# A streaming encoder step on one core: the order of the query tiles in the prompt's attention

## The chip, the cores and the metric

The kernel runs on one core of one Trainium2 chip. The core's engines work at the same time, each through its own list of instructions: TensorE (PE in the profile; its weight loads are PEld) multiplies matrices into PSUM, VectorE (DVE) and ScalarE (ACT) work elementwise and read PSUM, GpSimd (POOL) works elementwise in SBUF, and SyncE (SP) starts transfers. They meet by semaphores. The metric is the device time of the launch in microseconds (us), lower being better.

## The reference

One inference step of a two-layer encoder for a prompt of 1024 frames and eight running streams with 16 frames each. Layer 0 mixes by a gated linear recurrence, layer 1 by sparse attention, and each layer has a convolutional feed-forward part. Only the sparse attention on the prompt matters here:

```python
admissible = key_chunk[None, :] <= (pb // CHUNK)[:, None]        # chunks of 64 keys
score = jnp.where(admissible[None], score, -jnp.inf)             # from the indexer
sel_val, sel_idx = lax.top_k(score, n_sel)                       # n_sel = 256 for the prompt
logits = jnp.einsum('btkgd,btskd->btkgs', qg, kg) * scale        # 16 query heads, 4 key heads
p = jax.nn.softmax(logits, axis=-1)
o = jnp.einsum('btkgs,btskd->btkgd', p, vg)
```

A query sees its own chunk and the ones before, so a later query has more keys.

## The kernel before

The kernel is ten phases, one after the other. The phase that the diff touches, `attend_prompt_phase`, computes the prompt's attention with dense scores and a mask: `mask_p` holds 0 for the selected keys and -1e30 for the others.

The 1024 queries are eight tiles of 128 (`PT` = 8). Tile t sees (t+1) x 128 keys. The 16 heads are taken in pairs, one head in each half of the partitions, so a tile has `QB` = 8 blocks. Four blocks (`GROUP` = 4) are a group; a tile has two groups. The list `blocks` sets the order of the 64 blocks on every engine, and `groups` that of the 16 groups. Scores are written to PSUM in pieces of at most 512 keys: tiles 0 to 3 have one piece, tiles 4 to 7 have two.

A block passes the engines in this way (lines of the kernel before):

- GpSimd and ScalarE split the queries into a high and a low part (`split_q`, L2174, and L2097), six blocks ahead.
- TensorE makes the scores of both heads (`scores`, L2111 to L2115): three products a piece and head, high by high, low by high, high by low.
- VectorE adds the mask and takes the row maximum on the way out of PSUM (`maxima`, L2254), then the negative of it (`ap_neg_max`, L2263). Two pieces need one more instruction to join their maxima (L2260).
- ScalarE takes the exponentials and their sum (L2206).
- TensorE transposes the probabilities, 128 keys at a time (`turn`, L2124), and ScalarE copies them out of PSUM (L2195), two blocks (`LAG`) after the scores.
- After a whole group TensorE multiplies by the values (`values`, L2141) in parts, spread over the four blocks that follow. The sums are inverted, spread and multiplied in (L2267, L2131, L2271, L2150, L2179, L2278).

Between blocks, two searches for the top 256 are still going on, and their steps stand at fixed block numbers. Those on VectorE: twelve parts that settle the masks of tiles 6 and 7 (`finish_prompt`, in blocks 0 to 11); ten steps of the samples' search (`decide_samples`, in blocks 1 to 14, each after a pass of ScalarE over 2064 scores, `sign_samples`, L1779); and seven parts that settle the samples' mask (`finish_samples`, in blocks 28 to 34). The masks of tiles 0 to 5 are ready when the phase begins (`SEARCHED[-1]` is the pair of tiles 6 and 7).

The queries of a tile are loaded from device memory by SyncE into one of two buffers, when the tile two places before has been split.

Of the kernel before, what the change touches and what calls it, by code (L numbers as in the profile page):

```python
# [19 lines left out]
ALU = mybir.AluOpType  # L20
ACT = mybir.ActivationFunctionType
AX = mybir.AxisListType
F32 = mybir.dt.float32
# [4 lines left out]
P = 128  # L28
# [9 lines left out]
PT = NT - 1  # L38
# [29 lines left out]
class Space:  # L68
# [5 lines left out]
    def take(self, name, shape, dtype=F32, at=None):  # L74
        size = int(np.prod(shape[1:])) * (2 if dtype == BF16 else 4)
        size = (size + 31) // 32 * 32
        if at is None:
            at = self.at
            self.at += size
            assert self.at <= self.end, (name, self.at - self.end)  # L80
        t = self.nc.alloc_sbuf_tensor_at(name, list(shape), dtype, offset=at)
        t_at[name] = at
        return t
# [1064 lines left out]
GROUP = N_HEADS // N_KV  # L1148
QB = N_HEADS // 2
# [517 lines left out]
SEARCHED = (tuple(range(FIRST_TOP, FIRST_TOP + 2)), tuple(range(FIRST_TOP + 2, FIRST_TOP + 4)), tuple(range(FIRST_TOP + 4, PT)))  # L1667
# [349 lines left out]
def attend_prompt_phase(nc, env, x):  # L2017


    io, const, sem, tick = env["io"], env["const"], env["sem"], env["tick"]  # L2020
# [12 lines left out]
    q, q_hi, q_lo = take("ap_q", [P, 2, QB, P]), take("ap_q_hi", [P, QB, P], F32R), take("ap_q_lo", [P, QB, P], F32R)  # L2033
    k_hi = take("ap_k_hi", [P, 2, T_PROMPT], F32R)
    k_lo = take("ap_k_lo", [P, 2, T], F32R, at=t_at["at_k"])
# [4 lines left out]
    inv_rows, inv_of = idle("ap_inv_rows", [2 * GROUP, GROUP, P]), idle("ap_inv_of", [P, GROUP, P])  # L2040
    sel_half = idle("ap_sel_half", [2 * GROUP, P])
    own_head = take("ap_own_head", [2 * GROUP, GROUP])
    blocks = [(t, j) for t in range(PT) for j in range(QB)]
    groups = [(t, p) for t in range(PT) for p in range(2)]


    LAG, TAIL, AHEAD = 2, GROUP, QB - 2
# [8 lines left out]
    def scores_up_to(n):  # L2056
        return score_pieces[n][-1][0] + 1
# [10 lines left out]
    with ExitStack() as ctx:  # L2068
# [3 lines left out]
        q_in = [sem(f"ap_q_in{n}") for n in range(2)]  # L2072
        consts_in = sem("ap_consts_in")
        k_hi_set, q_hi_set, q_lo_set = sem("ap_k_hi_set"), sem("ap_q_hi_set"), sem("ap_q_lo_set")
# [7 lines left out]
        @block.sync  # L2082
        def _(sp):
            sp.dma_start(sel_half[:, :], io["sel_half"]).then_inc(consts_in, 16)
            sp.dma_start(own_head[:, :], io["own_head"]).then_inc(consts_in, 16)
            for t in range(PT):
                if t >= 2:
                    sp.wait_ge(q_lo_set, QB * (t - 1))
                sp.dma_start(q[:, t % 2], io["q_t"][:, :, t * P:(t + 1) * P].rearrange("j p t -> p j t")).then_inc(q_in[t % 2], 16)

        @block.gpsimd
        def _(pool):
            pool.wait_ge(k_hi_set, 1)
            pool.tensor_tensor(k_lo[:, :, 0:T_PROMPT], k_sb[:, :, 0:T_PROMPT], k_hi[:, :, :].bitcast(F32), ALU.subtract)
            for n, (t, j) in enumerate(blocks):
                pool.wait_ge(q_hi_set, n + 1)
                pool.tensor_tensor(q_lo[:, j], q[:, t % 2, j], q_hi[:, j].bitcast(F32), ALU.subtract).then_inc(q_lo_set, 1)  # L2097

        @block.tensor
        def _(pe):  # L2100
            def scores(n, c):
                t, j = blocks[n]
                k, a, e = score_pieces[n][c]
                pe.wait_ge(q_lo_set, n + 1)
                if k >= 2:
                    pe.wait_ge(qk_read, 2 * (k - 1))
                outs = [qk[half][k % 2][:, 0:e - a] for half in range(2)]
                rows = [slice(half * HEAD_D, (half + 1) * HEAD_D) for half in range(2)]
                keys = (j // GROUP, slice(a, e))
                for half in range(2):  # L2110
                    pe.matmul(outs[half], q_hi[rows[half], j, :], k_hi[(rows[half], *keys)], start=True, stop=False)  # L2111
                for half in range(2):
                    pe.matmul(outs[half], q_lo[rows[half], j, :], k_hi[(rows[half], *keys)], start=False, stop=False)
                for half in range(2):
                    i = pe.matmul(outs[half], q_hi[rows[half], j, :], k_lo[(rows[half], *keys)], start=False, stop=True)  # L2115
                i.then_inc(qk_done, 1)

            def turn(n, half):
# [49 lines left out]
        def _(act):  # L2168
            def split_q(n):
                t, j = blocks[n]  # L2170
                act.wait_ge(q_in[t % 2], 16 * (t // 2 + 1))
                if t:
                    act.wait_ge(qk_done, scores_up_to(n - QB))
                act.activation(q_hi[:, j], q[:, t % 2, j], ACT.Copy).then_inc(q_hi_set, 1)  # L2174

            def copy_inv(u):
                act.wait_ge(inv_done, u + 1)
# [4 lines left out]
            for n in range(QB):  # L2182
                split_q(n)
            for n in range(len(blocks) + LAG + TAIL):
                m, e = n - LAG, n - 1
                for half in range(2):
                    if 0 <= m < len(blocks):
                        t, j = blocks[m]
# [10 lines left out]
                    if 0 <= e < len(blocks):  # L2199
                        t, j = blocks[e]  # L2200
                        keys, u = (t + 1) * P, e // GROUP
# [604 lines left out]
```

## Time and profile before

| | us |
|---|---|
| median of three runs | 3840.33 (3840.1 to 3844.03) |
| the profiled execution | 3843.01 |
| its span | 3841.5 |
| TensorE busy in the span | 3543.3 (92%) |
| VectorE busy | 2126.6 (55%) |
| ScalarE busy | 1170.3 (30%) |
| the phase, first scores to last outputs | 2304.8 to 2607.5 |

The span is what the profiler saw between the first and the last instruction; the profiled execution's own time has some 1.5 us around it. Busy times are sums of the instructions' durations on an engine, with overlap counted once. A stretch of the span can be asked for by itself: that gives each engine's busy time in it, the number of instructions, and the clock that was granted to TensorE (1.00 is 2.4 GHz, 0.50 is 1.2 GHz). The timeline lists instructions by their start, and what an engine waited for stands in brackets.

### The profile page before, as it was taken

The page shows a single profiled execution, that of the slowest core. Times are in us where ns is not written, and L with a number is a line of the kernel's source. Part 1 is how long each engine was busy: PE and PEld are TensorE (multiplying, and loading weights), DVE is VectorE, ACT ScalarE, POOL GpSimd, SP SyncE. Part 2 cuts the span into 40 slices and gives each one's busy share as a digit, 9 for nine tenths or more (in the row PEclk, how much of TensorE's full clock was granted, in tenths as well). Part 3 has the DMA queues.
Part 4 walks back from the last instruction along what each step waited for, and adds up shares of the span by engine and source line. Part 5 has one row for each costly group of instructions (what it writes and reads, how often), then busy time and mean ns, then how long its engine had stood idle before and what let it go on. Part 6 is the DMA issues. An engine that isn't in the chain of part 4 may idle for free. (4 is left out here: it accounts for less than half of the span.)

```text
span 3841.5 us, 55603 instructions
## 1 busy us (share of the span) xinstructions
PE 3543.3 (92%) x19764; PEld 3152.8 (82%) x19780; DVE 2126.6 (55%) x3935; ACT 1170.3 (30%) x1961; POOL 224.4 (6%) x349
## 2 busy tenths in 40 slices
PE   5999999998999999999888977897889999999997
PEld 4988888986899999999853873453459999999996
DVE  5465555564555455545688666762232554555456
ACT  4222333322311111113236857673333111111112
POOL 3000000001000000002000001100002000000001
PEclk8888888887999999999958987999999999999998
DMA  2110011110111111111102220003431111111111
GB/s 89 34 40 29 30 39 40 34 40 12 41 45 44 40 45 45 39 40 55 68 12 88 70 71 23 12 1 151 160 124 41 40 43 39 45 45 40 40 45 63
DMA packets 57407, 192.23 MB, mean 50 GB/s; under 512 B 7016, under 2 KB 23408, under 8 KB 52528
## 3 DMA queue, kind: packets, MB, share of 16 engines
q1 hardware_dynamic: 52992, 167.89, 12.9%
q0 software_dynamic: 4144, 20.71, 1.5%
q8 instruction: 173, 2.83, 0.3%
q14 instruction: 98, 0.80, 0.1%
HBM read 166.64 MB, written 21.93 MB: 49 GB/s over the span
## 5 line engine op out<-in xcount | busy, mean ns | idle before, releaser
L292 PE MATMUL ff1lin<-ff1h_hi,ff1w_hi 128*128 128x384 f32 x1056 | 354.7, 336 | 9.9 <-DVE ff1w_lo L286 5.7
L292 PE MATMUL ff0lin<-ff0h_hi,ff0w_hi 128*128 128x384 f32 x1056 | 354.1, 335 | 7.2 <-DVE ff0w_lo L286 4.4
L293 PE MATMUL ff1lin<-ff1h_lo,ff1w_hi 128*128 128x384 f32 x1056 | 353.7, 335 | 0.0
L294 PE MATMUL ff1lin<-ff1h_hi,ff1w_lo 128*128 128x384 f32 x1056 | 353.6, 335 | 0.0
L293 PE MATMUL ff0lin<-ff0h_lo,ff0w_hi 128*128 128x384 f32 x1056 | 353.3, 335 | 0.0
L294 PE MATMUL ff0lin<-ff0h_hi,ff0w_lo 128*128 128x384 f32 x1056 | 353.3, 335 | 0.0
L292 PE MATMUL hg_lin<-hg_h_hi,hg_w_hi 128*128 128x384 f32 x768 | 269.6, 351 | 17.4 <-POOL hg_h_lo L165 15.4
L293 PE MATMUL hg_lin<-hg_h_lo,hg_w_hi 128*128 128x384 f32 x768 | 264.3, 344 | 0.0
L294 PE MATMUL hg_lin<-hg_h_hi,hg_w_lo 128*128 128x384 f32 x768 | 263.4, 343 | 0.0
L292 PEld LDWEIGHTS ff1lin<-ff1h_hi,ff1w_hi 128*128 128x128 f32 x1056 | 199.0, 188 | 12.7 <-DVE ff1w_lo L286 6.3
L292 PEld LDWEIGHTS ff0lin<-ff0h_hi,ff0w_hi 128*128 128x128 f32 x1056 | 198.8, 188 | 8.5 <-DVE ff0w_lo L286 4.7
L293 PEld LDWEIGHTS ff1lin<-ff1h_lo,ff1w_hi 128*128 128x128 f32 x1056 | 199.0, 188 | 0.1
L294 PEld LDWEIGHTS ff1lin<-ff1h_hi,ff1w_lo 128*128 128x128 f32 x1056 | 198.9, 188 | 0.0
L293 PEld LDWEIGHTS ff0lin<-ff0h_lo,ff0w_hi 128*128 128x128 f32 x1056 | 198.8, 188 | 0.1
L294 PEld LDWEIGHTS ff0lin<-ff0h_hi,ff0w_lo 128*128 128x128 f32 x1056 | 198.7, 188 | 0.0
L1099 DVE TENSOR_TENSOR x<-x,ff1lin 128x384 f32<-128x384 f32 x264 | 141.1, 553 | 102.3 <-PE ff1lin L294 99.9
L1099 DVE TENSOR_TENSOR x<-x,ff0lin 128x384 f32<-128x384 f32 x264 | 141.1, 553 | 101.6 <-PE ff0lin L294 99.2
L292 PE MATMUL ff1lin<-ff1y_hi,ff1w_hi 128*128 128x384 f32 x528 | 180.0, 341 | 2.5 <-DVE ff1w_lo L286 2.5
L292 PE MATMUL ff0lin<-ff0y_hi,ff0w_hi 128*128 128x384 f32 x528 | 179.9, 341 | 2.5 <-DVE ff0w_lo L286 2.5
L294 PE MATMUL ff1lin<-ff1y_hi,ff1w_lo 128*128 128x384 f32 x528 | 180.1, 341 | 0.0
L293 PE MATMUL ff1lin<-ff1y_lo,ff1w_hi 128*128 128x384 f32 x528 | 180.0, 341 | 0.0
L293 PE MATMUL ff0lin<-ff0y_lo,ff0w_hi 128*128 128x384 f32 x528 | 179.7, 340 | 0.0
(429 smaller groups left out, 7806.3 us busy)
## 6 DMA issues: line engine op xcount, KB each, us to landing
ff_raw<-in_weights SPq DMA_DIRECT2D x132, 512.0 KB, 3.6
hg_raw<-in_weights SPq DMA_DIRECT2D x40, 512.0 KB, 3.5
as_keys<-in_cache_k SPq DMA_DIRECT2D x16, 1024.0 KB, 4.9
as_vals<-in_cache_v SPq DMA_DIRECT2D x8, 2048.0 KB, 9.2
se_keys<-in_cache_ki SPq DMA_DIRECT2D x8, 1024.0 KB, 5.0
pb_raw<-in_weights SPq DMA_DIRECT2D x12, 512.0 KB, 3.5
x<-in_x SPq DMA_DIRECT2D x3, 1536.0 KB, 9.1
x_keep<-x POOLq DMA_DIRECT2D x1, 4608.0 KB, 18.6
```

Of the source, the lines that this page charges most:

```text
L292: pe.matmul(out, w_hi, x_hi, start=start, stop=False)
L293: pe.matmul(out, w_hi, x_lo, start=False, stop=False)
L294: return pe.matmul(out, w_lo, x_hi, start=False, stop=stop)
L1099: dve.tensor_tensor(xs, xs, lin[n % 6][:, 0:GT], ALU.add).then_inc(down_out, 1)
```

## The change

The tiles are taken in another order. Tiles 5 and 0 come first, a group of four blocks of one and a group of the other in turns, then 4 and 1, then 3 and 2; tiles 6 and 7 stay last, whole tile by whole tile. Everything that was addressed by the tile's number or the pair's number and depended on the old order (the two query buffers, the split queries, the waits for them) is addressed by the place in the new order.

```diff
-    blocks = [(t, j) for t in range(PT) for j in range(QB)]
-    groups = [(t, p) for t in range(PT) for p in range(2)]
+    order = [t for n in range(SEARCHED[-1][0] // 2) for t in (SEARCHED[-1][0] - 1 - n, n)] + list(SEARCHED[-1])
+    place = {t: n for n, t in enumerate(order)}
+    groups = [(t, p) for n in range(0, PT - 2, 2) for p in range(2) for t in order[n:n + 2]] + [(t, p) for t in SEARCHED[-1] for p in range(2)]
+    blocks = [(t, GROUP * p + n) for t, p in groups for n in range(GROUP)]
...
-            for t in range(PT):
-                if t >= 2:
-                    sp.wait_ge(q_lo_set, QB * (t - 1))
-                sp.dma_start(q[:, t % 2], io["q_t"][:, :, t * P:(t + 1) * P].rearrange("j p t -> p j t")).then_inc(q_in[t % 2], 16)
+            for n, t in enumerate(order):
+                if n >= 2:
+                    sp.wait_ge(q_lo_set, blocks.index((order[n - 2], QB - 1)) + 1)
+                sp.dma_start(q[:, n % 2], io["q_t"][:, :, t * P:(t + 1) * P].rearrange("j p t -> p j t")).then_inc(q_in[n % 2], 16)
...
-                pool.tensor_tensor(q_lo[:, j], q[:, t % 2, j], q_hi[:, j].bitcast(F32), ALU.subtract).then_inc(q_lo_set, 1)
+                pool.tensor_tensor(q_lo[:, n % QB], q[:, place[t] % 2, j], q_hi[:, n % QB].bitcast(F32), ALU.subtract).then_inc(q_lo_set, 1)
...
-                    pe.matmul(outs[half], q_hi[rows[half], j, :], k_hi[(rows[half], *keys)], start=True, stop=False)
+                    pe.matmul(outs[half], q_hi[rows[half], n % QB, :], k_hi[(rows[half], *keys)], start=True, stop=False)
...
-                act.wait_ge(q_in[t % 2], 16 * (t // 2 + 1))
-                if t:
+                act.wait_ge(q_in[place[t] % 2], 16 * (place[t] // 2 + 1))
+                if n >= QB:
                     act.wait_ge(qk_done, scores_up_to(n - QB))
-                act.activation(q_hi[:, j], q[:, t % 2, j], ACT.Copy).then_inc(q_hi_set, 1)
+                act.activation(q_hi[:, n % QB], q[:, place[t] % 2, j], ACT.Copy).then_inc(q_hi_set, 1)
```

How this moves the instructions is seen in the engines' lists. VectorE at the start of the phase, before (`ap_probs,ap_part_max` is the masked maximum of one head; the second row of it reads the accumulator; `ap_above` is the first part of the search for tile 6):

```order
L2254 ISA ap_probs,ap_part_max<-ap_bank,mask_p 128x128
L2254 ISA ap_part_max 128x1
L2263 TENSOR_SCALAR ap_neg_max<-ap_part_max 128x1
L2254 ISA ap_probs,ap_part_max<-ap_bank,mask_p 128x128
L2254 ISA ap_part_max 128x1
L2263 TENSOR_SCALAR ap_neg_max<-ap_part_max 128x1
L1785 TENSOR_SCALAR ap_above,sp_count<-score_p,sp_cand 128x896
```

And the same place now:

```order
L2256 ISA ap_probs,ap_part_max<-ap_bank,mask_p 128x512
L2256 ISA ap_part_max 128x1
L2256 ISA ap_probs,ap_part_max<-ap_bank,mask_p 128x512
L2256 ISA ap_part_max 128x1
L2256 ISA ap_probs,ap_part_max<-ap_bank,mask_p 128x256
L2256 ISA ap_part_max 128x1
L2262 TENSOR_TENSOR ap_part_max<-ap_part_max 128x1
L2265 TENSOR_SCALAR ap_neg_max<-ap_part_max 128x1
L2256 ISA ap_probs,ap_part_max<-ap_bank,mask_p 128x256
L2256 ISA ap_part_max 128x1
L2262 TENSOR_TENSOR ap_part_max<-ap_part_max 128x1
L2265 TENSOR_SCALAR ap_neg_max<-ap_part_max 128x1
```

The first block before the search's first part was tile 0's and is now tile 5's, in two pieces.

VectorE around the samples' finish, blocks 30 and 31, before (`mask_s`, `ss_` and `score_s` are the samples' search):

```order
L1748 TENSOR_SCALAR mask_s,ss_count<-score_s,ss_cand 128x2064
L1749 TENSOR_SCALAR ap_ties<-score_s,ss_cand 128x2064
L1751 TENSOR_SCALAR ss_need<-ss_count 128x1
L2271 TENSOR_TENSOR ap_inv_rows<-ap_bank,ap_own_head 8x512
L2254 ISA ap_probs,ap_part_max<-ap_bank,mask_p 128x512
L2254 ISA ap_part_max 128x1
L2263 TENSOR_SCALAR ap_neg_max<-ap_part_max 128x1
```

And now:

```order
L1748 TENSOR_SCALAR mask_s,ss_count<-score_s,ss_cand 128x2064
L1749 TENSOR_SCALAR ap_ties<-score_s,ss_cand 128x2064
L1751 TENSOR_SCALAR ss_need<-ss_count 128x1
L2273 TENSOR_TENSOR ap_inv_rows<-ap_bank,ap_own_head 8x512
L2256 ISA ap_probs,ap_part_max<-ap_bank,mask_p 128x256
L2256 ISA ap_part_max 128x1
L2265 TENSOR_SCALAR ap_neg_max<-ap_part_max 128x1
```

The same parts at the same block numbers, beside tile 1 (256 keys) in place of tile 3 (512 keys).

TensorE in block 6, where the values of the first group begin, before (`ap_probs_t` holds the transposed probabilities of the group; `c_ident` marks a transpose):

```order
L2111 MATMUL ap_bank<-ap_k_hi,ap_q_hi 128x128 x2
L2113 MATMUL ap_bank<-ap_k_hi,ap_q_lo 128x128 x2
L2115 MATMUL ap_bank<-ap_k_lo,ap_q_hi 128x128 x2
L2141 MATMUL ap_bank<-ap_probs_t_13278,at_v 64x512 x2
L2124 MATMUL ap_bank<-c_ident,ap_probs 128x128 x2
```

And now, blocks 6 and 7:

```order
L2113 MATMUL ap_bank<-ap_k_hi,ap_q_hi 128x128 x2
L2115 MATMUL ap_bank<-ap_k_hi,ap_q_lo 128x128 x2
L2117 MATMUL ap_bank<-ap_k_lo,ap_q_hi 128x128 x2
L2143 MATMUL ap_bank<-ap_probs_t_13278,at_v 64x512 x4
L2126 MATMUL ap_bank<-c_ident,ap_probs 128x128
L2143 MATMUL ap_bank<-ap_probs_t_13278,at_v 64x512 x2
L2126 MATMUL ap_bank<-c_ident,ap_probs 128x128
L2113 MATMUL ap_bank<-ap_k_hi,ap_q_hi 128x128 x2
L2115 MATMUL ap_bank<-ap_k_hi,ap_q_lo 128x128 x2
L2117 MATMUL ap_bank<-ap_k_lo,ap_q_hi 128x128 x2
L2143 MATMUL ap_bank<-ap_probs_t_13278,at_v 64x512 x2
```

The values of the long tile (five pairs in these two blocks; a pair is one product for each head) stand beside the short tile's scores, where one pair stood.

## Rows read from the trace of the kernel before

**Rows 1.** Busy time by stretch: us, PE, PEld, DVE, ACT, POOL, clock, DMA.

```profile
2304.80:2317.30 12.50, 6.25 (x36) 4.52 (x36) 9.41 (x41) 11.02 (x27) 3.32 (x9) 0.50 0.15 42
2317.30:2332.70 15.40, 10.05 (x37) 4.63 (x38) 11.21 (x38) 9.19 (x31) 1.80 (x4) 0.50 0.01 2
2332.70:2349.80 17.10, 10.13 (x44) 4.98 (x42) 13.99 (x46) 12.80 (x34) 1.83 (x4) 0.60 0.11 31
2349.80:2363.70 13.90, 12.21 (x56) 6.03 (x57) 7.98 (x36) 12.25 (x37) 2.02 (x5) 0.66 0.00 1
2363.70:2373.90 10.20, 8.76 (x53) 4.26 (x49) 6.65 (x27) 7.66 (x27) 1.63 (x4) 1.00 0.19 53
2373.90:2387.10 13.20, 12.29 (x65) 6.36 (x64) 6.89 (x28) 9.93 (x32) 1.83 (x4) 0.87 0.00 1
2387.10:2400.70 13.60, 12.36 (x70) 6.09 (x70) 7.88 (x28) 10.54 (x30) 1.83 (x4) 1.00 0.14 40
2400.70:2421.90 21.20, 15.63 (x79) 7.06 (x78) 17.73 (x41) 11.76 (x32) 2.63 (x5) 0.92 0.00 1
2421.90:2447.20 25.30, 20.92 (x113) 11.29 (x111) 20.46 (x57) 13.69 (x36) 2.60 (x4) 0.80 0.08 21
2447.20:2464.30 17.10, 16.23 (x107) 8.72 (x105) 11.47 (x51) 12.54 (x35) 1.83 (x4) 1.00 0.01 2
2464.30:2483.30 19.00, 18.16 (x118) 9.80 (x116) 12.58 (x51) 14.47 (x37) 1.82 (x4) 1.00 0.10 28
2483.30:2502.70 19.40, 18.49 (x121) 10.14 (x119) 12.72 (x52) 15.16 (x38) 1.83 (x4) 1.00 0.00 1
2502.70:2607.50 104.80, 102.77 (x614) 53.02 (x613) 58.16 (x209) 76.28 (x156) 4.59 (x10) 1.00 0.00 1
```

**Rows 2.** Timeline of VectorE, the two heads of a block: start us, duration us, instruction.

```profile
2320.16 0.29 DVE L2254 CUSTOM_DVE_ANT_0 ap_probs<-ap_bank,mask_p 128x128 f32<-128x128 f32 x1 [0.54 <-issue]
...
2320.63 0.29 DVE L2254 CUSTOM_DVE_ANT_0 ap_probs<-ap_bank,mask_p 128x128 f32<-128x128 f32 x1
...
2440.33 0.28 DVE L2254 CUSTOM_DVE_ANT_0 ap_probs<-ap_bank,mask_p 128x128 f32<-128x128 f32 x1
...
2441.03 0.29 DVE L2254 CUSTOM_DVE_ANT_0 ap_probs<-ap_bank,mask_p 128x128 f32<-128x128 f32 x1
```

**Rows 3.** Groups by shape on VectorE: count, busy us, mean ns, idle before.

```profile
L2254 DVE CUSTOM_DVE_ANT_0 ap_probs<-ap_bank,mask_p 128x512 f32<-128x512 f32 x96 | 65.5, 691 | 43.6 <-PE ap_bank L2124 23.9 <-PE ap_bank L2115 18.8 <-issue 0.5
...
L2254 DVE CUSTOM_DVE_ANT_0 ap_probs<-ap_bank,mask_p 128x256 f32<-128x256 f32 x32 | 13.6, 424 | 7.8 <-PE ap_bank L2124 4.0 <-PE ap_bank L2115 2.6 <-issue 0.9
...
L2271 DVE TENSOR_TENSOR ap_inv_rows<-ap_bank,ap_own_head 8x512 f32<-8x512 f32 x16 | 10.7, 671 | 0.8 <-PE ap_bank L2131 0.5 <-issue 0.2
L2278 DVE TENSOR_TENSOR o_t<-ap_bank,ap_inv_of 128x512 f32<-128x512 f32 x16 | 10.4, 649 | 8.7 <-PE ap_bank L2141 8.7
```

**Rows 4.** The same view for ScalarE's copies of the transposed probabilities.

```profile
L2195 ACT ACTIVATE ap_probs_t<-ap_bank 128x512 f32<-128x512 f32 x96 | 56.0, 602 | 47.7 <-PE ap_bank L2124 47.3
...
L2195 ACT ACTIVATE ap_probs_t<-ap_bank 128x256 f32<-128x256 f32 x32 | 12.3, 385 | 4.1 <-PE ap_bank L2124 4.0
...
L2195 ACT ACTIVATE ap_probs_t<-ap_bank 128x128 f32<-128x128 f32 x32 | 8.7, 273 | 0.7 <-PE ap_bank L2124 0.6
```

**Rows 5.** Timeline of TensorE in tile 7 (eight transposes, scores, one value pair).

```profile
2560.02 1.09 PE L2124 MATMUL ap_bank<-c_ident,ap_probs 128*128 128x128 f32 x8
2561.04 0.50 PE L2111 MATMUL ap_bank<-ap_k_hi,ap_q_hi 64*128 64x512 f32 x2
...
2561.95 1.08 PE L2141 MATMUL ap_bank<-ap_probs_t,at_v 128*64 128x512 f32 x4
2562.95 1.09 PE L2124 MATMUL ap_bank<-c_ident,ap_probs 128*128 128x128 f32 x8
```

**Rows 6.** DMA issues in the phase: count, KB each, median us to landing.

```profile
ap_q<-q_t SPq DMA_DIRECT2D x8, 512.0 KB, 4.0
```

**Rows 7.** Busy time by stretch, in the select phase (columns as in rows 1).

```profile
1926.10:2030.00 103.90, 89.43 (x234) 62.93 (x234) 88.08 (x234) 35.96 (x76) 0.00 (x0) 0.50 0.00 1
```

More of the change, by code:

```diff
@@ L2110, in scores @@
                 for half in range(2):
-                    pe.matmul(outs[half], q_hi[rows[half], j, :], k_hi[(rows[half], *keys)], start=True, stop=False)
+                    pe.matmul(outs[half], q_hi[rows[half], n % QB, :], k_hi[(rows[half], *keys)], start=True, stop=False)
                 for half in range(2):
-                    pe.matmul(outs[half], q_lo[rows[half], j, :], k_hi[(rows[half], *keys)], start=False, stop=False)
+                    pe.matmul(outs[half], q_lo[rows[half], n % QB, :], k_hi[(rows[half], *keys)], start=False, stop=False)
                 for half in range(2):
-                    i = pe.matmul(outs[half], q_hi[rows[half], j, :], k_lo[(rows[half], *keys)], start=False, stop=True)
+                    i = pe.matmul(outs[half], q_hi[rows[half], n % QB, :], k_lo[(rows[half], *keys)], start=False, stop=True)
                 i.then_inc(qk_done, 1)
```

## The prediction

> **What bounds the kernel now.** I started from the page's first part, by which TensorE is busy for most of the span. The change touches one stage, the prompt attention, so the next view is the busy time by stretch, cut at the end of the last `ap_neg_max` of every group of four blocks [rows 1]. Below, group g0 is the first of those rows, and a block is one of 64 (a tile of 128 queries and one pair of heads); tile t has t+1 pieces of 128 keys. The reader is to see two kinds of rows. In g9 to g11 (tiles 4 and 5) TensorE is busy nearly throughout: 16.23 of 17.10, 18.49 of 19.40. In g0 to g2 (tiles 0, 0, 1) it is not: 6.25 of 12.50, 10.05 of 15.40, 10.13 of 17.10, and this at a granted clock of 0.50 to 0.60. There VectorE has 9.41, 11.21 and 13.99, the rest being short gaps between dependent instructions: the first twelve blocks also carry the twelve parts that finish the search for the last two tiles' masks. The same happens in g7 and g8 (tiles 3 and 4; VectorE 17.73 of 21.20, 20.46 of 25.30), where the samples' search is finished. TensorE's busy time multiplied by the clock adds up, over g0 to g11, to about 138 us of 197.9, so at most some 60 us could be had if nothing but TensorE counted.
>
> The stage's timeline then gives VectorE's price of a block, and the groups by shape those of single instructions [rows 2 to 5].
>
> **The change, step by step.** No instruction is added that counts; the blocks come in another order, and the searches' parts stay at their block numbers. So the same extra VectorE work now lies beside other tiles. I go through the groups in the new order: tiles 5, 0, 5, 0, 4, 1, 4, 1, 3, 2, 3, 2.
>
> Blocks 0 to 11 (tiles 5, 0, 5). Before, these twelve numbers took 12.50 + 15.40 + 17.10 = 45.0 us, set by VectorE, with maxima of eight blocks of tile 0 and four of tile 1. A half of a tile-0 block takes 2320.63 - 2320.16 = 0.47 us from start to start [rows 2], 0.18 more than its reduction's 0.29; for tile 1 that is 0.42 + 0.18 = 0.60 [rows 3]. So a block costs 0.94 and 1.20. A block of two pieces has two reductions of 512 at 0.69 [rows 3] and two last pieces; a last piece of 128 takes 2441.03 - 2440.33 = 0.70 [rows 2], one of 256 is 0.42 - 0.28 = 0.14 longer, 0.84. Tile 5 thus costs 1.38 + 1.68 = 3.06 a block. Now there are eight of tile 5 and four of tile 0: 24.5 + 3.8 = 28.3 against 7.5 + 4.8 = 12.3, so 16 us more on the engine that sets the pace: 61.0. TensorE's own work of tile 5 hides under it at full clock. To that I add: 1 us for the first scores, 512 columns wide (a piece takes 2561.95 - 2561.04 = 0.91 at full clock [rows 5], 1.8 at half, and the narrow one an estimated half of it); 3 us in blocks 4 to 7, which must still turn and evacuate two blocks of tile 5 (two 512 and two 256 evacuations each for two of 128, 2 x (2 x (0.60 + 0.39) - 2 x 0.27) = 2.9 us of ScalarE [rows 4], and 20 transposes at 1.02/8 = 0.13 and four value pairs at 1.0 = 6.6 us of TensorE at full clock [rows 5], 13 at half); 1.5 us for TensorE at half clock in blocks 8 to 11. Sum 66.5, against 45.0.
>
> Blocks 12 to 15 (tile 0, with tile 5 behind it). Before, g3 took 13.90 with ScalarE at 12.25 and two of the sign passes. Now ScalarE has 2.9 more for evacuations; what the last tile-5 block's exponentials add and the shorter tile saves I let cancel (an estimate): 15.1. TensorE has 8 us at full clock in g3 (12.21 x 0.66), 6.6 more for the tail of tile 5, and some 3 less for the shorter tile (eight transposes, one value pair, an estimated 1 for narrower scores): 11.6, or 23 at half clock. So 15.1 if the clock is full, 23 if not; I take 17.8, nearer the lower end, since in g3 the clock was on its way up (0.66).
>
> Blocks 16 to 27 (tiles 4, 1, 4). TensorE needs (16.23 + 7.1)/2 = 11.7 a group, 7.1 being the mean of 10.13 x 0.60 and 12.21 x 0.66 for tile 1. VectorE needs 4 x (1.38 + 1.40) = 11.1 for tile 4, and 0.67 + 0.65 and a reciprocal for the group's end [rows 3]: 12.6. So in the long groups VectorE is the slower, by 0.9, and ScalarE close by (12.54 in g9). I take 14.0 for each long group and 12.6 for the short one; the ends are 12.6 and 11.7 (no wait) and 17.10 and 13.90 (as each stood alone). Sum 40.6.
>
> Blocks 28 to 35 (tiles 1, 3). The samples' finish keeps its place. Before, g7 + g8 = 46.5 with tiles 3 and 4, set by VectorE; tile 4's maxima, 11.1, give way to tile 1's, 4.8: 40.2.
>
> Blocks 36 to 47 (tiles 2, 3, 2). TensorE at full clock: tile 3 (12.36 + 15.63 x 0.92)/2 = 13.4, tile 2 (8.76 + 12.29 x 0.87)/2 = 9.7, mean 11.6. In g4 and g6 it stood idle 1.44 and 1.24 us; with 1.4 more it is 13.0 a group, 39.0; with nothing lost it would be 34.8.
>
> Tiles 6 and 7 keep their order, 104.80 before. They now follow tile 2, so twelve transposes and three value pairs less hang over: 12 x 0.13 + 3 x 1.0 = 4.5. That makes 100.3.
>
> The sum: 66.5 + 17.8 + 40.6 + 40.2 + 39.0 + 100.3 = 304.4 against 302.7: 1.7 us longer. What is gained by smoothing TensorE's work (six short groups that it no longer starves through) is spent where VectorE now reduces tile 5 between the search's parts. The profiled execution took 3843.0 (span 3841.5), the runs' median is 3840.3; with 1.7 I come to 3844.7 for an execution like the profiled one and 3842 for the median.
>
> **Edits at nothing.** The query loads wait for a tile two places back in the new order; a load lands in 4.0 us [rows 6], and from the last use of tile 5's buffer (block 11's split, six blocks early) to the first split of tile 4 there are five blocks, none under 2.5 us (10.20/4). Uncovered, each of six loads would cost up to 4.0. The loads of the first two places are both needed before the first sign pass; before, it was so too. The index arithmetic issues nothing.
>
> **Rivals.** *The regimes overlap fully (faster).* VectorE-bound and TensorE-bound stretches mix and all coupling goes: blocks 0 to 11 at 62.0, then 15.1, 12.6 + 11.7 + 12.6, 40.2, 3 x 11.6, 100.3: 289.3, so 13.4 us less, 3827. For it: the two resources' sums in [rows 1]; against it: g4 to g6, which no search burdens, still leave TensorE idle 1.44, 0.91 and 1.24. The Trainium skill, page "Perfetto Trace Analysis", section "Optimization Strategy", says that where the most-contended engine changes over time, interleaving those regimes may improve performance. By that rule this rival's time comes out; the trace agrees that there are two regimes, but no run yet shows them mixed.
>
> *TensorE stays at half clock (slower).* Mechanism: between the search's parts TensorE has nothing to do, the clock stays at 1.2 GHz, and in blocks 4 to 7 (10.05 + 13) and 12 to 15 TensorE needs 23 each. Price: 23 for 18.4 in blocks 4 to 7, another 1.5 in blocks 8 to 11, 23 for 17.8 in blocks 12 to 15: 11.3 on top of the forecast, 3853. It decides if the clock is still 0.50 after block 12. For it: g0 to g3 run at 0.50 to 0.66, and in the select stage TensorE was busy 89.43 of 103.90 us and kept 0.50 throughout [rows 7]. Against: where tile 4 came (g8 to g9) the clock went from 0.80 to 1.00. The Trainium skill, page "TensorE: Matmul & The Clock Gate", section "Loop structure matters more than you think", says that the loop nest decides whether the matmuls stay warm. By that rule the order alone may cost this much; rows 7 agree in so far as a steadily fed but waiting TensorE stayed at half clock.
>
> *The loads come late, so the turns don't overlap.* Six loads at 4.0 each, 24 us, 3866. It would need blocks under 1 us.
>
> **How the numbers follow.** Forecast 49%, its own range 3835 to 3849 (the ends of blocks 4 to 7, 12 to 15 and of the long groups). Full overlap 21%, half clock 28%, late loads 2%. The range, 3828 to 3857, takes in most of both. What can be told from no change is 0.2%, 7.7 us: faster holds nearly all of the overlap case, 0.21; slower the half-clock case and the loads, 0.29; the forecast stays within it, 0.50.
>
> **What would show it.** Right: the first twelve blocks near 66 us with VectorE as releaser, groups of tiles 4 to 1 near 13 each, the rows for tiles 6 and 7 unchanged but for some 4 us. Wrong: a first stretch under 60 (VectorE's drains hide more than I think) or a clock of 0.50 past block 16; groups at 11.7 with TensorE full would show the overlap.

## The result and the profile after

The changed kernel took 3854.39 us (median of eight runs, 3846.22 to 3855.47) against 3844.17 for the kernel before on the same chip (eight runs, 3840.1 to 3846.1): 1.0023 of it, with an interval of 1.0014 to 1.0032. A second set gave 3852.59 against 3843.17, 1.0025 [1.0015, 1.0036]. So it is slower by some 10 us: inside the whole range given (3828 to 3857), but beyond the forecast's own (3835 to 3849), and on the slow side of the 0.2% within which the forecast had put it. As a bare number it lies nearest to the half-clock rival's 3853.

The profiled execution took 3855.03 us (span 3853.5). This is its changed stage, cut as in [rows 1]: tiles 5, 0, 5, 0, 4, 1, 4, 1, 3, 2, 3, 2, then tiles 6 and 7. The columns are those of [rows 1]: stretch and length, busy time of TensorE, its weight loads, VectorE, ScalarE and GpSimd, granted clock, DMA share and GB/s.

```profile
2307.30:2328.40 21.10, 15.69 (x84) 11.55 (x85) 16.48 (x64) 17.91 (x35) 3.77 (x9) 0.66 0.00 0
2328.40:2346.60 18.20, 13.28 (x61) 6.12 (x63) 10.98 (x38) 12.33 (x34) 1.56 (x3) 0.81 0.10 30
2346.60:2371.10 24.50, 19.30 (x104) 10.24 (x100) 20.46 (x70) 19.10 (x43) 3.17 (x5) 0.83 0.08 23
2371.10:2387.40 16.30, 13.63 (x60) 7.32 (x59) 6.83 (x35) 12.12 (x33) 1.36 (x3) 0.63 0.01 2
2387.40:2404.50 17.10, 16.01 (x102) 8.44 (x101) 11.40 (x52) 12.16 (x39) 2.29 (x5) 1.00 0.00 0
2404.50:2416.60 12.10, 9.79 (x60) 4.67 (x59) 5.85 (x28) 8.58 (x29) 1.36 (x3) 1.00 0.16 45
2416.60:2433.80 17.20, 16.05 (x106) 8.74 (x105) 11.26 (x52) 12.75 (x39) 2.28 (x5) 1.00 0.11 32
2433.80:2451.60 17.80, 12.76 (x60) 5.37 (x59) 15.61 (x41) 9.28 (x31) 1.82 (x4) 0.80 0.00 0
2451.60:2472.40 20.80, 17.45 (x68) 7.92 (x67) 16.57 (x33) 9.44 (x27) 1.37 (x3) 0.68 0.00 1
2472.40:2485.60 13.20, 11.79 (x70) 5.64 (x67) 6.87 (x28) 9.97 (x30) 1.83 (x4) 1.00 0.15 40
2485.60:2499.80 14.20, 12.96 (x72) 6.34 (x71) 7.87 (x28) 11.15 (x32) 1.83 (x4) 1.00 0.14 39
2499.80:2512.80 13.00, 11.74 (x69) 5.66 (x67) 6.88 (x28) 9.60 (x28) 1.84 (x4) 1.00 0.01 1
2512.80:2613.00 100.20, 98.57 (x592) 51.58 (x591) 57.33 (x209) 74.69 (x155) 5.03 (x11) 1.00 0.00 1
```

The reader should compare by tiles, not by row, and keep in mind that the searches' parts stand beside other tiles than before. Tiles 5 and 0 took 21.1 + 18.2 + 24.5 + 16.3 = 80.1 us; in [rows 1] tile 0 took 27.9 and tile 5 38.4, 66.3 in all. Tiles 4 and 1 took 64.2 where they had taken 73.4, tiles 3 and 2 61.2 for 58.2, the last row 100.2 for 104.8. The stage is 305.7 us long against 302.7. VectorE's instructions cost what they did ([rows 3]: a reduction of 512 is 689 ns here, 691 there), and the query loads land in 4.0 us as in [rows 6].

From the stage's first DMA issue to the next stage's it is 313.7 us against 310.0, and the stage behind it, whose code is the same, took 205.7 against 199.8. The stage also begins 2.5 us later (2300.3 against 2297.8) behind code that is the same; together this is the 12 us by which the two traces differ. In a second trace of the changed kernel (e9) the two stages took 317.4 and 202.8. So together they took 9.6 and 10.4 us more than before, about the difference of the medians.

How a stall in the first blocks looks: the timeline of the changed kernel in blocks 8 and 9 (start, length, engine, line, operation, out<-in; weight loads and other rows left out).

```profile
2352.77 0.66 PE L2126 MATMUL ap_bank<-c_ident,ap_probs 128*128 128x128 f32 x4
...
2353.35 2.02 ACT L1779 ACTIVATE mask_s<-score_s,ss_cand 128x2064 bf16<-128x2064 f32 x1 [0.64 <-DVE ss_cand L1732]
2353.43 1.28 DVE L1748 TENSOR_SCALAR_CACHE_REDUCE mask_p<-score_p,sp_cand 128x1024 bf16<-128x1024 f32 x1
...
2355.37 0.26 ACT L2197 ACTIVATE ap_probs_t<-ap_bank 128x128 f32<-128x128 f32 x1
...
2355.68 0.63 PE L2126 MATMUL ap_bank<-c_ident,ap_probs 128*128 128x128 f32 x2 [2.25 <-ACT ap_probs_t L2197]
...
2357.39 0.79 PE L2113 MATMUL ap_bank<-ap_k_hi,ap_q_hi 64*128 64x512 f32 x2
```

TensorE has turned probabilities into a bank at 2353.4; the copy that empties the bank stands on ScalarE behind a sign pass of the samples' search, 2.02 us long, which itself waited 0.64 us for its threshold. TensorE waits 2.25 us for the copy. Afterwards a pair of 512-column score matmuls takes 0.79 us; in a later block of tile 4, at a clock of 1.00, it is this:

```profile
2428.96 0.50 PE L2113 MATMUL ap_bank<-ap_k_hi,ap_q_hi 64*128 64x512 f32 x2
```

### The profile page after: what moved, and what is told of

Read it like the earlier page. It is cut to its first block and busy times, and to the rows that moved or that the text cites. A ratio compares the mean times of both kernels' runs of the same rounds, so it can differ in the third digit from the quotient of the medians.

```text
span 3853.5 us, 55602 instructions
## 1 busy us (share of the span) xinstructions
PE 3558.5 (92%) x19764; PEld 3159.3 (82%) x19780; DVE 2124.9 (55%) x3935; ACT 1171.7 (30%) x1961; POOL 224.4 (6%) x349
## 3 DMA queue, kind: packets, MB, share of 16 engines
q1 hardware_dynamic: 52992, 167.89, 12.9%
## 5 line engine op out<-in xcount | busy, mean ns | idle before, releaser
L292 PEld LDWEIGHTS ff1lin<-ff1h_hi,ff1w_hi 128*128 128x128 f32 x1056 | 199.0, 188 | 12.1 <-DVE ff1w_lo L286 6.3
L294 PEld LDWEIGHTS ff0lin<-ff0h_hi,ff0w_lo 128*128 128x128 f32 x1056 | 198.7, 188 | 0.0
L1099 DVE TENSOR_TENSOR x<-x,ff0lin 128x384 f32<-128x384 f32 x264 | 141.1, 553 | 100.3 <-PE ff0lin L294 97.9
L294 PE MATMUL ff0lin<-ff0y_hi,ff0w_lo 128*128 128x384 f32 x528 | 179.2, 339 | 0.0
```

What stands on the lines that cost most here:

```text
L292: pe.matmul(out, w_hi, x_hi, start=start, stop=False)
L294: return pe.matmul(out, w_lo, x_hi, start=False, stop=stop)
L1099: dve.tensor_tensor(xs, xs, lin[n % 6][:, 0:GT], ALU.add).then_inc(down_out, 1)
```

## The experiments

The experiments vary three things: the order of the tiles, ScalarE's ten sign passes (blocks 0 to 13), and VectorE's nineteen parts that finish the two searches (twelve in blocks 0 to 11, seven in blocks 28 to 34). "Stage" is from its first DMA issue to the next stage's; stretches end with a group's last `ap_neg_max` and begin 7.0 us after the first issue; the rows above are cut up to 0.2 us earlier. Stretches and stages are from one trace each. The last column is the unchanged stage behind. The kernel before was run beside each set and had medians of 3842.3 to 3844.2; ratios are to that.

| kernel | blocks 0–15 | 0–47 | stage | median | behind |
|---|---|---|---|---|---|
| before | 59.0 | 198.0 | 310.0 | 3844.2 | 199.8 |
| changed | 80.3 | 205.6 | 313.7 | 3854.4 | 205.7 |
| e9, changed once more | 81.6 | 209.3 | 317.4 | 3852.6 | 202.8 |
| e3, before, no parts | 51.7 | 178.0 | 290.0 | 3823.8 | 201.4 |
| e4, changed, no parts | 75.9 | 191.5 | 299.6 | 3832.3 | 200.0 |
| e6, before, neither | 41.2 | 168.6 | 280.4 | 3817.2 | 204.1 |
| e5, changed, neither | 59.3 | 174.8 | 283.0 | 3818.9 | 204.9 |
| e7, changed, no passes | 65.5 | 189.2 | 297.2 | 3832.5 | 202.4 |
| e1, first pair turned | 73.1 | 198.7 | 306.8 | 3840.0 | 205.3 |
| e2, parts by short tiles | 77.5 | 197.1 | 305.2 | 3839.6 | 201.2 |
| e8, e1 with late parts | 72.9 | 187.2 | 306.3 | 3840.4 | 203.5 |
| e11, e1 with parts spread | 73.0 | 203.1 | 311.1 | 3844.5 | 202.3 |
| e10, before, parts spread | 59.4 | 209.0 | 321.0 | 3855.2 | 200.1 |
| e12, e1 and e2 together | 70.7 | 196.3 | 304.4 | 3837.3 | 202.0 |

**e3 and e4: both orders without VectorE's parts.**

```diff
-                    part, at = divmod(u - 1, 2)
-                    if at == 0 and 0 <= part < len(PROMPT_PARTS):
-                        finish_prompt(*PROMPT_PARTS[part])
                     part, at = divmod(u - finish_at, 2)
-                    if at == 0 and 0 <= part < FINISH_PARTS:
+                    if at == 0 and part == 0:
+                        ...
+                    if at == 0 and part == FINISH_PARTS - 1:
                         finish_samples(part)
```

> The kernel before with the parts that finish the two searches left out (the masks of tiles 6 and 7 and of the samples are set to zero by three memsets at block 28, so the output isn't the reference's); order of tiles as before. Blocks 0 to 11 lose twelve parts of about 2.7 us: from 45.0 to 20 if VectorE alone set them, to some 30 if TensorE at half clock and ScalarE's sign passes are next; blocks 28 to 35 go from 46.5 to about 31. Total some 30 us under the kernel before, about 3814. It is the other half of the next run.

> The changed kernel with the same parts left out in the same way (output isn't the reference's). It tells what the order of tiles does where no search stands beside it. Theory A (the turns do gain, and VectorE's parts beside tile 5 eat the gain): at least 5 us below the run without the parts in the order of before. Theory C (the turns themselves gain nothing, since a long group takes as long after a short one as after a long one): within 3 us of that run. Theory B (half clock in the first blocks): above it by 3 us or more, with a granted clock near 0.6 in blocks 0 to 15.

Three memsets in block 28 (1.8 us) stand in for the parts, and the last and smallest of the seven (0.5 us) stays. Measured: 0.9942 [0.9929, 0.9956] and 0.9965 [0.9951, 0.9979] of before; e4's stage is 9.6 us longer than e3's. e3 gained less than expected: 3823.8 for 3814, with 34.7 us in blocks 0 to 11 and 35.2 in blocks 28 to 35. In e4 the sign is theory B's, but the clock in blocks 0 to 15 is 0.75 and not near 0.6. Theory A, on which the prediction's largest term rested, falls: with the parts gone the first twelve blocks of the order in turns still take 58.7 us (63.9 with them), with VectorE busy for half of it. The stretch of blocks 0 to 15 in the changed kernel, in e4 and in e3:

```profile
2307.30:2387.40 80.10, 61.89 (x304) 35.23 (x305) 54.76 (x205) 61.46 (x143) 9.86 (x20) 0.74 0.05 14
```

```profile
2304.30:2380.20 75.90, 60.59 (x305) 34.20 (x305) 35.50 (x172) 61.42 (x143) 8.81 (x20) 0.75 0.05 15
```

```profile
2303.50:2355.20 51.70, 41.49 (x170) 21.07 (x171) 22.53 (x125) 45.47 (x127) 9.22 (x21) 0.54 0.07 21
```

From the first to the second row VectorE loses 19.3 us of work and the stretch 4.2. ScalarE is busy 61.4 us in both, as long as TensorE is at this clock (61.9 and 60.6), and the clock is nearly the same. That pointed at ScalarE's sign passes.

**e5, e6 and e7: the sign passes out.** The conditions before `sign_samples` and `decide_samples` become `False`, so VectorE's ten short decisions go too; e5 and e6 leave out the parts too, e7 keeps them.

> The changed kernel without the parts that finish the searches and also without the samples' ten sign passes on ScalarE (20.2 us in the run without the parts) and their decisions on VectorE; three memsets stand in, so the output isn't the reference's. In the run without the parts blocks 0 to 15 still took 75.9 us, with VectorE busy 35.5 and ScalarE 61.4 of it. Theory D (ScalarE's sign passes beside tile 5 set these blocks): 75.9 falls by most of the passes' 22 us, to about 56. Theory B (TensorE's half clock sets them, and the passes are covered): it stays above 68, at a granted clock under 0.85. Theory C (long and short blocks in turns hold each other up in any case): it falls to no less than 66, at full clock.

> The kernel before with the same left out (the output isn't the reference's). Its blocks 0 to 15 (tiles 0 and 1) took 51.7 us without the parts, with ScalarE busy 45.5. Theory D: with the sign passes gone too they fall by most of 22 us, to about 32. Theory B: TensorE at half clock keeps them above 42. It is the other half of the run before it: by theory C the order in turns stays the slower one here as well (by about 10 us over the whole phase); by theory D the order in turns is then level or faster, since what hurt it was the search beside tile 5.

> The changed kernel with the parts that finish the searches, but without the ten sign passes and their decisions (the output isn't the reference's). The prediction took VectorE's sum alone for blocks 0 to 11 (theory A): by it they lose only the decisions and stay near 58 of 63.9. By theory D they fall to about 50, since ScalarE was the engine next to full (18.1 of 21.3 and 19.2 of 24.5 us in the two groups of tile 5).

Measured: 0.9938 [0.9921, 0.9955], 0.9931 [0.9916, 0.9946] and 0.9978 [0.9968, 0.9988] of before. Blocks 0 to 15 in e5, e7 and e6:

```profile
2307.30:2366.60 59.30, 52.90 (x305) 29.80 (x305) 32.68 (x152) 41.35 (x123) 8.73 (x20) 0.86 0.07 19
```

```profile
2299.80:2365.30 65.50, 52.84 (x305) 30.43 (x305) 50.60 (x186) 41.93 (x123) 8.93 (x20) 0.87 0.06 17
```

```profile
2305.20:2346.40 41.20, 38.94 (x162) 20.14 (x163) 18.61 (x104) 25.25 (x104) 8.79 (x20) 0.54 0.09 26
```

Theory D holds in the main for blocks 0 to 15 of the order in turns: taking the passes out saves 16.6 us (75.9 to 59.3) or, with the parts in, 14.8 (80.3 to 65.5); taking VectorE's parts out saves 4.4 to 6.2. In blocks 0 to 11, for which e7 had been forecast, it holds by half: 54.6 us, where theory A gave 58 and theory D 50. There the parts alone add 8.8 us to e5's 45.8, and the passes alone 12.9. The waits say by which path the passes cost: TensorE's turns for ScalarE's copies, in blocks 0 to 15 of the changed kernel and of e7 (us in total, times, longest).

```profile
PE ap_bank L2126 <- ACT ap_probs_t L2197: 15.0, 10, 3.7
```

```profile
PE ap_bank L2126 <- ACT ap_probs_t L2197: 4.4, 6, 1.1
```

That isn't all of it. In the rows above, TensorE's idle time falls from 18.2 us to 12.7 (its waits for VectorE grow by some 5), and its busy time for the same products from 61.9 to 52.8, at a clock of 0.87 in place of 0.74. From e4 to e5 idle falls by 8.9 and busy by 7.7. So about half of what the passes cost or more is time at a lower clock, which is theory B's side of it; whether the passes bring the clock down by making TensorE wait was not tested by itself. Passes and parts are coupled as well: ScalarE's passes wait 6.0 us for VectorE's thresholds in the changed kernel, and 2.0 in e4.

In the order of before the same passes cost 10.5 (51.7 to 41.2), less than theory D expected; e6's row shows why. With tiles 0 and 1 alone TensorE is busy 38.9 of 41.2 us at a clock of 0.54: theory B's half clock is what is left there. With the passes in (e3) TensorE is idle 10.2 us in place of 2.3, so about half of their 20 us was covered.

e5 and e6 also answer whether the turns gain anything by themselves. Tiles 4, 1, 4 and 1 in e5:

```profile
2366.60:2383.70 17.10, 16.01 (x103) 8.56 (x102) 11.42 (x53) 12.16 (x39) 2.30 (x5) 1.00 0.00 0
2383.70:2395.80 12.10, 9.79 (x60) 4.54 (x57) 5.85 (x27) 8.59 (x29) 1.36 (x3) 1.00 0.17 46
2395.80:2413.00 17.20, 16.05 (x106) 8.86 (x106) 11.25 (x53) 12.73 (x39) 2.30 (x5) 1.00 0.11 31
2413.00:2427.90 14.90, 12.69 (x60) 5.56 (x58) 7.56 (x31) 8.73 (x29) 1.36 (x3) 0.77 0.00 1
```

And tiles 1 and 4 in e6, each by itself:

```profile
2320.20:2332.70 12.50, 11.99 (x44) 5.74 (x43) 5.76 (x28) 7.14 (x29) 1.82 (x4) 0.50 0.15 42
2332.70:2346.40 13.70, 13.03 (x54) 5.85 (x53) 5.64 (x27) 7.83 (x31) 1.82 (x4) 0.63 0.00 1
...
2400.60:2418.30 17.70, 17.64 (x117) 9.79 (x117) 11.62 (x55) 14.19 (x39) 2.28 (x5) 1.00 0.11 31
2418.30:2435.40 17.10, 16.22 (x107) 8.59 (x106) 11.16 (x51) 12.38 (x35) 1.83 (x4) 1.00 0.00 1
```

61.3 us in turns, 61.0 one after the other; for tiles 3 and 2 it is 54.2 and 54.2, for tiles 5 and 0 59.3 and 53.4. (The last group in turns took 14.90 at a clock of 0.77; in e8, below, it took 12.1 at 1.00.) Only the last two tiles are shorter in turns, by 3.8, since a short tile hangs over into them. The Trainium skill, page "Perfetto Trace Analysis", section "Optimization Strategy", says that interleaving regimes bound by different engines may improve performance. The traces of these two runs do not bear it out: with no search beside them, the turns gain nothing in any pair.

With these runs the stage's 3.7 us can be split (each from one trace; the two traces of the changed kernel differ by 3.7 themselves):

| | order of before | in turns | difference |
|---|---|---|---|
| neither | 280.4 | 283.0 | +2.6 |
| sign passes (e3 − e6, e4 − e5) | +9.6 | +16.6 | +7.0 |
| VectorE's parts (before − e3, changed − e4) | +20.0 | +14.1 | −5.9 |
| sum | 310.0 | 313.7 | +3.7 |

For the order in turns the other sequence gives the same (16.5 for the passes and 14.2 for the parts, by e7); for the order of before it was not run. The ratios of all runs give 2.7 us for the first row, 6 for the passes and nothing for the parts, which cost 22 in either order (0.58%). Each of these ratios is known to some 0.15%, 6 us, so they do not show how the difference splits; the −5.9 in particular is one trace's, and 2.7 of it is the group just named, at 0.77 in e4 too. What both ways agree in: without VectorE's parts the order in turns is still the slower by 8 to 10 us, and with the passes out as well 2 to 3 are left, which is within the noise.

**e1: the first pair turned, short tile first.**

```diff
-    order = [t for n in range(SEARCHED[-1][0] // 2) for t in (SEARCHED[-1][0] - 1 - n, n)] + list(SEARCHED[-1])
+    order = [0, 5, 4, 1, 3, 2] + list(SEARCHED[-1])
```

> As the changed kernel, but the first pair of tiles is taken short one first: the groups come as tiles 0, 5, 0, 5, 4, 1, 4, 1, 3, 2, 3, 2. The twelve search parts keep blocks 0 to 11, which now hold four blocks of tile 5 and eight of tile 0, where the changed kernel has eight and four. If VectorE's sum sets these blocks (theory A, the prediction's): 4 x (3.06 - 0.94) = 8.5 us less there, 63.8 to about 55; blocks 12 to 15 become tile 5 and blocks 16 to 19 carry its tail, some 3 us more; so blocks 0 to 19 go from 97.2 to about 92 and the kernel is some 5 us under the changed one, about 3849. If TensorE at half clock sets them (theory B): the same matmuls lie in blocks 0 to 15, so blocks 0 to 15 stay within 3 us of 80.1 and the kernel stays at 3852 to 3856.

0.9987 [0.9978, 0.9997] of before: 14 us under the changed kernel where theory A gave 5 and theory B none. Blocks 0 to 15 are 7.2 us shorter (73.1), the sign of theory A; but e4 has shown that VectorE's sum isn't the cause. The passes stand five beside either tile in both orders, so they don't tell the two apart; four of VectorE's parts beside tile 5 in place of eight do, but all twelve were worth only 4.4 us in the changed kernel. It is no chance: e8 and e11 begin in the same way and took 72.9 and 73.0. Part of it is that tile 5's last turns and values now fall behind block 15. Blocks 0 to 47 hold the same matmuls in both orders; the changed kernel and e1:

```profile
2307.30:2512.90 205.60, 170.55 (x897) 88.00 (x897) 137.17 (x489) 144.49 (x391) 24.48 (x52) 0.85 0.06 16
```

```profile
2301.50:2500.20 198.70, 163.20 (x897) 84.12 (x897) 137.86 (x489) 143.58 (x390) 28.25 (x52) 0.87 0.06 17
```

TensorE is idle for 35.1 and 35.5 us, so the whole 6.9 us is its busy time, at a clock that is higher on the whole. Why this order gets the higher clock is open, and so is the rest of the 14 us: the stage has 6.9 of them, 10.6 against e9.

**e2: VectorE's parts only beside short tiles.**

```diff
+                    prompt_at = [2 * b + 1 for b in (4, 5, 6, 7, 12, 13, 14, 15, 20, 21, 22, 23)]
+                    if u in prompt_at:
+                        finish_prompt(*PROMPT_PARTS[prompt_at.index(u)])
+                    samples_at = [2 * b for b in (28, 29, 30, 31, 36, 37, 38)]
+                    if u in samples_at:
+                        finish_samples(samples_at.index(u))
```

> As the changed kernel, same order of tiles, but the parts that finish the two searches stand only beside short tiles: the twelve of the last two tiles' masks in blocks 4 to 7, 12 to 15 and 20 to 23 (tiles 0, 0, 1), the seven of the samples' in blocks 28 to 31 and 36 to 38 (tiles 1 and 2). Theory A (VectorE pays for tile 5 and the search's parts in the same blocks): blocks 0 to 11 fall from 63.8 to about 48, blocks 16 to 27 rise from 46.4 to about 51, blocks 28 to 39 fall from 51.8 to about 47.5: some 15 us less, about 3839, and under the kernel before. Theory B (TensorE at half clock sets the first sixteen blocks, whatever VectorE does): blocks 0 to 15 stay at 75 or more, and the kernel stays within 5 us of the changed one.

0.9988 [0.9979, 0.9997]; 3839.55 where 3839 was expected, but by another way: blocks 0 to 11 fell only to 58.4, the level without any parts (58.7), though four parts remain there, blocks 16 to 27 went from 46.4 to 44.9 where 51 was expected, and blocks 28 to 39 fell to 47.6, as expected. Blocks 12 to 15, with four parts now, rose from 16.3 to 19.1, so blocks 0 to 15 took 77.5: above 75, as theory B had it. Four parts beside tile 1 were free: its group took 12.3 us with them and 12.1 without.

**e8, e10, e11: other places for the samples' seven parts.** In e8, beside tiles 6 and 7 (`finish_at = 2 * blocks.index((SEARCHED[-1][0], GROUP - 1))`); in e10 and e11 e2's edit with other numbers.

> The order 0, 5, 0, 5, 4, 1, 4, 1, 3, 2, 3, 2, and the seven parts that finish the samples' search moved from blocks 28 to 34 to blocks 51 to 57, beside tiles 6 and 7, where VectorE was busy 55.6 of 85.1 us and TensorE all of it. If the parts are hidden there: blocks 28 to 35 go from 37.3 to the 28.7 of the run without the parts, and all else stays: 8 us under the 3840 of the first such order, about 3831. If each part holds up its block's maxima and through them TensorE, half of 7 x 2.2 us comes back in the last two tiles: about 3838.

> The kernel before, with the seven parts that finish the samples' search at every second block from 16 to 28 (tiles 2 and 3) in place of every block from 28 to 34 (tiles 3 and 4); they are 1.3 to 4.5 us each, some 18 in all, on VectorE. Without the parts blocks 28 to 35 took 35.0 where they take 46.5 with them: 11.5 us to be had there. If a part beside two short blocks is covered (VectorE has 3.3 us of work in two blocks of tile 2, which last 5.2 to 6.5), blocks 16 to 27 grow by 3 us or less and the kernel comes 8 us under before, 3835. If each part holds up TensorE by half its length, as beside tiles 6 and 7 (10.9 of 18), 9 us comes back and the kernel stays within 3 us of before.

> The order 0, 5, 0, 5, 4, 1, 4, 1, 3, 2, 3, 2, with the samples' seven parts at every second block of the short tiles alone: blocks 20, 22, 28, 30, 36, 38 and 44 (tiles 1 and 2). In this order they cost 11.7 us at blocks 28 to 34 (37.3 against 25.6) and 10.9 beside tiles 6 and 7. By the theory that what counts is VectorE's share beside the part, a part beside a short tile (5.9 us of VectorE in groups of 12.1 to 13.5) is half covered: some 6 us under that order's 3840, about 3834. If a part costs its length wherever it stands, 3840 again.

e8 is 0.9996 [0.9987, 1.0005], nearer the second of its two figures. Blocks 28 to 35 fell from 37.3 to 25.6, but tiles 6 and 7 (to the last `ap_neg_max`) rose from 85.1 to this:

```profile
2489.20:2585.20 96.00, 87.41 (x523) 47.80 (x524) 73.96 (x223) 68.06 (x143) 10.91 (x11) 0.96 0.00 1
```

VectorE's 18.3 us more cost 10.9, although it had 29 to spare: the maxima of the next block stand in its list behind a part, of which the longest instruction takes 4.45 us. ScalarE then waits for the maxima, 11.9 us in seven times, where in e1's last two tiles it waits once for 0.3:

```profile
ACT ap_probs L2208 <- DVE ap_neg_max L2265: 11.9, 7, 3.8
```

e10 is 1.0040 [1.0027, 1.0054], 12 us slower than before, where 8 faster or level was expected: blocks 16 to 27 went from 37.0 to 61.4, at clocks of 0.83, 0.74 and 0.76. e11 is 1.0005 [0.9996, 1.0014], 3844.5 where 3834 or 3840 was expected. So the same parts cost 8.4 us (e2, against the 39.2 of e8 in blocks 28 to 39), 11 to 12 (e1, e8), and over blocks 16 to 47 12.6 (before, against e3), 15.8 (e11, against e8) or 23.2 (e10, against e3). In these two pairs parts spread out were dearer than parts in a row. Each figure is from one trace, and the clock is in it: of e10's 23.2 us TensorE's busy time, for the same products, has 10.6.

**e9: the changed kernel once more.**

> The changed kernel itself once more. Between the first two traces the changed stage grew by 3.7 us (310.0 to 313.7), and the stage behind it, the samples' attention, whose code is the same, by 5.9 (199.8 to 205.7), with its first matmuls at a granted clock of 0.50 in place of 0.75. Over the ten traces so far that stage took from 199.8 to 205.7, and not by the order of tiles (200.0 and 204.9 with the order in turns, 199.8 and 204.1 with the order of before). If it is chance of the execution (theory E), the second trace may show any value from 199 to 206 there, the changed stage again 313 to 315, and the medians differ by about 4 to 6 us. If it belongs to the change (theory F), the stage behind shows 205 again and the medians differ by 9 to 11.

The median repeats (9.4 us over before), as theory F said; the stage behind took 202.8, as theory E said, and the changed stage 317.4, as neither did. Most of the 3.7 more is one group of tile 1, the same instructions as the 12.10 us row above at another clock, together with 1.5 in blocks 12 to 15:

```profile
2401.20:2416.00 14.80, 12.60 (x60) 5.37 (x57) 5.84 (x27) 8.68 (x29) 1.36 (x3) 0.77 0.14 37
```

**e12: e1 and e2 together.**

> The two versions that came out under the kernel before, put together: the order 0, 5, 0, 5, 4, 1, 4, 1, 3, 2, 3, 2, and the searches' parts only beside short tiles: the twelve of the last two tiles' masks in blocks 0 to 3, 8 to 11 (tile 0) and 20 to 23 (tile 1), the seven of the samples' in blocks 28 to 31 and 36 to 38 (tiles 1 and 2). If parts cost little beside short tiles: blocks 4 to 7 go from 22.2 to about 18, blocks 20 to 23 from 13.5 to about 15, blocks 28 to 39 from 50.5 to the 47.6 that the same placing gave in the order with tile 5 first: some 6 us under 3840, about 3834. If each part costs much the same wherever it stands, it stays at 3838 to 3842.

3837.33 (3832.41 to 3845.77), 0.9989 [0.9980, 0.9998]: the lowest median of the kernels that compute everything, 5 us under before. By its ratio it is no better than e1 or e2 alone (0.9987 and 0.9988): the two do not add up. It lies between the two forecasts. Blocks 4 to 7 took 20.4, blocks 20 to 23 13.8; of the 2.9 us expected in blocks 28 to 39 none came, since the group of tile 2 took 17.8 at a clock of 0.81 (14.8 at 1.00 in e2). So the seven parts, placed as in e2, cost 11.4 us here against e8, where they had cost 8.4.

## Why the prediction was right in sum and wrong in cause

- **Blocks 0 to 11: 66.5 forecast, 63.8 measured.** The size is nearly right, the step under it is wrong: "61.0" from VectorE's sum, with VectorE as releaser. Without the twelve parts it is 58.7. In blocks 0 to 15 TensorE waited 15.0 us for ScalarE's copies and 2.9 for VectorE. The sign passes, which the prediction never priced as a term of their own, are worth 14.8 to 16.6 us in blocks 0 to 15 of this order, 9.3 to 12.9 of them in blocks 0 to 11. The reading to learn from is the ScalarE column: it was in the rows (11.02 of 12.50 in g0, [rows 1]), fuller there than VectorE's 9.41. The waits of the kernel before, blocks 0 to 15, say the same; this is TensorE's longest once the stage has begun:

```profile
PE ap_bank L2124 <- ACT ap_probs L2206: 17.6, 10, 5.1
```

- **Blocks 12 to 15: 17.8 forecast, 16.3 measured** (17.9 in e9), at a clock of 0.63 to 0.59: between the two ends given, as chosen.
- **Blocks 16 to 27: 40.6 forecast, 46.4 measured.** This is the term that was mis-sized, twice over. The step "TensorE needs (16.23 + 7.1)/2 = 11.7 a group" gives 23.3 for a long and a short group together; the rows after have 16.01 + 9.79 = 25.8. The 7.1 for tile 1 was busy time at a low clock multiplied by that clock, and that is too little: 25.8 less the 16.2 of tile 4 leaves 9.6. And the pair does not share its time evenly: 17.1 and 12.1, not 14.0 and 12.6, in a stretch with two long groups and one short. The long groups stand at the upper end that was given for them, the pair's 29.2 close to the 30.8 that the two take by themselves in e6 (13.70 and 17.10). TensorE is idle 2.3 of 12.1 us in the short group and 1.1 of 17.1 in the long one.
- **Blocks 28 to 35: 40.2 forecast, 38.6 measured; blocks 36 to 47: 39.0 and 40.4; tiles 6 and 7: 100.3 and 100.2.** These sizes held.
- **The stage's sum, +1.7 forecast, is +3.0** by the same cut (+3.7 from issue to issue, +7.4 in e9). That it came so close is luck: the terms miss by −2.7, −1.5, +5.8, −1.6, +1.4 and −0.1 and cancel. What was said of its cause, smoothing paid for by VectorE's parts, does not hold: with all search work out the turns gain nothing (+2.6), and without VectorE's parts the order in turns is still slower, by 9.6 in the stage. In the traces the sign passes cost more beside tile 5 (+7.0) and VectorE's parts less (−5.9); the ratios leave both open.
- **Outside the stage.** The prediction gave the stage behind no term. It took 5.9 and 3.0 us more, which is much of why the median lies 10 to 12 us above the 3842 forecast for it. Its first 6 us of matmuls, before and after:

```profile
2615.80:2621.80 6.00, 5.94 (x19) 1.27 (x19) 2.10 (x6) 0.00 (x0) 0.00 (x0) 0.75 0.98 414
```

```profile
2622.00:2628.00 6.00, 4.87 (x10) 0.90 (x11) 1.11 (x3) 0.00 (x0) 0.00 (x0) 0.50 0.98 416
```

  After the pause for its first loads the clock rose later in the changed kernel's trace. Over fourteen traces this stage took 199.8 to 205.7 with no clear relation to the order of tiles (200.0 in e4, 204.1 in e6). Whether the change makes the late rise likelier is open.
- **The rivals.** Full overlap did not come. The half clock did not last past block 16: the rival as stated, 23 us each in blocks 4 to 7 and 12 to 15, was wrong (18.2 and 16.3). Its nearness to the measured time is chance, since at most 7.4 of the 10 us are in the stage. But a clock below full is in every stretch that holds search work, 0.63 to 0.83 in blocks 0 to 15, 0.80 and 0.68 in blocks 28 to 35, and it is a good part of what the sign passes cost. The loads were not late, but for one wait. The prediction says that the first two loads are both needed before the first sign pass, as before. Before, the eight splits ahead of that pass were all tile 0's and needed one load; now four are tile 5's and four tile 0's, and ScalarE waits for the second load:

```profile
2307.05 0.91 ACT L2176 ACTIVATE ap_q_hi<-ap_q 128x128 fp32r<-128x128 f32 x4 [0.79 <-DMA ap_q<-q_t]
```

## What to carry to other kernels

Before interleaving long and short work, sum each engine's busy time over the pair, every engine and every pass that stays at its block number: here ScalarE's column held the largest cost of the first sixteen blocks, and it had no term. In this kernel, interleaving moved only what the pipeline lets hang over (3.8 us at the last two tiles). A long string of instructions costs by what stands behind it in its engine's list and by what becomes of the clock: eighteen microseconds of VectorE cost 8 to 23 in six placings, and 8.4 and 11.4 in the same one. Before a split of a few microseconds is believed, the same kernel has to be traced twice.

## What was not expected of the hardware

The same matmuls, those of the group of tile 0 behind tile 5, took 10.9 us at a granted clock of 1.00 (e7), 13.5 at 0.75 (e5) and 16.3 at 0.63 (the changed kernel, with passes beside it). In e7 and e5:

```profile
2354.40:2365.30 10.90, 8.80 (x53) 4.31 (x53) 5.79 (x29) 7.31 (x29) 1.36 (x3) 1.00 0.00 0
```

```profile
2353.10:2366.60 13.50, 11.78 (x55) 5.82 (x53) 4.74 (x27) 7.84 (x28) 1.36 (x3) 0.75 0.01 2
```

e7 carries more VectorE work than e5 and is faster here: the difference is 2.6 us, more than the 1.7 that the prediction forecast for the whole stage, and TensorE's busy time has all of it (8.80 against 11.78). The Trainium skill, page "TensorE: Matmul & The Clock Gate", section "Loop structure matters more than you think", says that the loop nest decides whether matmuls stay warm. The traces agree in part: the clock changed with the tiles and with the search work (0.74 over blocks 0 to 15 of the changed kernel, 0.57 before, 0.86 without search work). But TensorE's idle time does not tell it: blocks 20 to 23 of the changed kernel ran at 1.00 with 2.3 us idle of 12.1, blocks 12 to 15 at 0.63 with 2.7 of 16.3. And two executions of one kernel differ in it (12.10 and 14.80 us for one group).
